# Second block of a two-block kernel: gate chain, output scaling and row product in another order on VectorE, w_hi one panel ahead at both norms, mean squares in two parts

## The chip, the cores and the metric

One core of a Trainium2 chip runs the whole kernel as one launch. The metric is the device time of an execution in microseconds (us); lower is better. The kernel before took 987.55 us, the median of three runs (987.34 to 988.13).

The engines are named as in the profile: PE is TensorE (matmuls), DVE is VectorE, ACT is ScalarE, POOL is GpSimd, SP issues most of the loads. Each works through its own queue of instructions in the order in which they were written, and waits on semaphores for the others.

## The reference, cut to what matters

The input is 256 tokens of 1024 features. A first block (modulated norm, gated spatial unit, state space scan, MLP) is followed by a second block. The change touches the end of the first block and the second one:

```
x = first_block(...)                     # ends with: rms_norm(x, final_norm_w)
xn = rms_norm_2(x, attn_norm_g)
proj = xn @ w_in                         # q, k, v of MoBA and GLA, gates; gate_lr is 16 wide
log_a = log_sigmoid(gate_lr @ w_gate_up + b_gate) / 16
og = gla_attention(gq, gk, gv, log_a)    # gated linear attention with decays exp(cumsum(log_a))
...                                      # MoBA attention, gating of og
x = x + concat([y_moba, y_gla]) @ w_out
hn = rms_norm_2(x, ffn_norm_g)
h = causal_dwconv(hn @ w_ffn_up, conv_w, conv_b)     # 3 taps, 5632 channels
x = x + (silu(h_gate) * h_val) @ w_ffn_down
return rms_norm_2(x, final_norm_g)
```

## The kernel before, in words

**Layout and weights.** Activations lie with features on the 128 partitions and the 256 tokens along the free axis. All large products are taken in three matmuls, since each operand is split into a high part in a reduced format and the rest: high x high, high x low, low x high (`panel`, L1443). The weights come as panels of 128 x 1024 numbers, four at a time in the slots of `raw`. For each panel SP loads `raw`, ACT converts it to `w_hi` (`split_hi`, L442), DVE subtracts to get `w_lo` (`split_lo`, L840), then PE takes it: 24 matmuls of 256 columns. `w_hi` of a slot may be written again once PE has finished the slot's former panel (semaphore `used`); `raw` once DVE has taken it (`taken`). A chunk is four panels, one output of 512 features for 256 tokens in half of `proj_ps`.

**Order.** It is written out by hand for each engine. Nothing is scheduled by a tool, so an instruction waits for all that stands ahead of it on its engine.

**The stage in2** (the second block's input projection; `i2` is its first chunk). So that PE need not wait for the norm, the first chunk is computed from unnormalised input (`pre2_hi`, `pre2_lo`) and scaled by the row of inverse root mean squares afterwards. The mean squares are matmuls with one column (`mean_square`, L1494, line of the matmul L1504); their inverse roots are put on a diagonal (`diag`, `broadcast`, L886) and spread over all partitions by one matmul with ones (`row_of`, L1509, matmul L1512); ACT copies the row to `rr_sb` (`row_scale`, L479). DVE and ACT then make the normalised input `act_hi`, `act_lo` in pairs of tiles (`norm_apply`, L894; `norm_hi`, L493), and in between each converts the next chunk's panels. There are two rows in this stage: row 2 is the second block's norm with the first block's final norm folded in, row 3 is the first block's final norm itself. Row 3 is used by `first_output` (L1221), which scales the residual `xres` in eight instructions, and is needed only when the second block's first residual is added, much later.

**The gate chain.** PE multiplies the 16 wide projection with `wgu` (L1761). DVE adds the bias and takes the absolute value (L1228, L1230), ACT takes exp(-|x|) (L724), DVE adds 1 (L1244), ACT takes the logarithm (L727) and exp of its negative (L729), DVE corrects rounding (`softplus_lost`, `softplus_add`, L919 to L923), forms log_sigmoid (L1250), divides by 16 (L1252) and takes a cumulative sum over the tokens (L1255, `glog`).

**The levels.** The decayed scores are computed in eight levels of block size 1 to 128. For level e DVE forms differences of `glog` in `gd` (`level_diff`, L1265), ACT takes exponentials (L719, L720), POOL multiplies queries and keys by them into `gx` (L424, L426), PE takes the level product (`level_mm`, L1788) and DVE picks the entries that belong to the level into `scores_t` (L1279). PE runs one level product behind each panel of the third and fourth chunk; product 0 uses `gqk` as it is, product 1 needs the first `gx`.

**The stage up** (`up`, eleven chunks) begins like in2: a first chunk from unnormalised input, mean squares, one row (row 4), the norm in pairs. Its first chunk is scaled into `up0` (L1392). Three convolution taps follow per chunk: the last one on ACT (`last_tap`, L566), the two earlier ones on DVE in two pairs of tiles (L1045), then a SiLU on ACT, the product on DVE (L1397) and the split into `glu_hi` and `glu_lo`. PE may write a half of `proj_ps` again once the taps of the chunk that lay there are done (`fc_done`).

## Time and profile before

| | |
|---|---|
| median of the runs | 987.55 us (987.34 to 988.13) |
| the profiled execution | 987.19 us |
| its span, first to last instruction | 985.5 us |
| busy, share of the span | PE 951.7 us (97%), DVE 696.0 (71%), ACT 528.2 (54%), POOL 149.8 (15%) |
| mean granted clock of PE | 0.983 of full speed |
| single operations, us | `w_lo` 1.2, next one 1.14 later; `w_hi` 1.05; table load on ACT 1.28; row copy on ACT 0.37; `diag` 0.42; `xres` scaling, 4 in a row, 1.65; memset of `scores_t` 1.34; memset of ones 0.48; scaling by 1/16 0.42; first `gd` 0.69 |
| a panel on PE at full clock | 24 matmuls, 0.12 us apart, some 2.9 us |

How to read it: the span is what the hardware profiler saw of one execution; about 1.7 us lie around it. In a timeline row the first number is the start in us from the span's start, the second the duration, xN says how many instructions a row merges, and the bracket at the end gives the engine's idle time before the row and whom it waited for. A duration of a matmul is longer than its distance to the next, since they are pipelined. The two passes of a matmul on full 32 bit numbers (mean squares, rows, level products) are counted one by one in the profile.

### The profile page before, as it was taken

Reading aid. Unit: us, or ns where it says so; the run is one execution under the profiler, and the core shown is the slowest. Engines: PE = TensorE matmul, PEld = TensorE weight load, DVE = VectorE, ACT = ScalarE, POOL = GpSimd, SP = SyncE. Lnnn points to the kernel's source line nnn. Section 1 sums busy time; section 2 is a strip of 40 time slices with the busy share of each in tenths; the row PEclk is TensorE's granted clock in tenths of the full one; section 3 lists DMA queues with packets and bytes.
Section 4 is the critical chain, followed back from the end, with each engine's and each line's share of the span. In section 5 each row is a group of like instructions: output and inputs, shape, how many; then the busy total and the mean of one; then the engine's idle time right before and its main releaser. Section 6 shows DMA issues by size and latency. Waiting matters only on the chain.

```text
span 985.5 us, 19172 instructions
## 1 busy us (share of the span) xinstructions
PE 951.7 (97%) x7452; PEld 902.4 (92%) x7452; DVE 696.0 (71%) x911; ACT 528.2 (54%) x715; POOL 149.8 (15%) x118
## 2 busy tenths in 40 slices
PE   8999999989999999999999999998998989999997
PEld 5799999979989899989999999987877989999996
DVE  5937877887899977566665454598765678877553
ACT  3466555555565664455555353564365666566442
POOL 0100000254786611000000020004300000000010
PEclk9999999999999999999999999998999999999999
DMA  9845445576676746535555646334323346556551
GB/s 347 340 154 167 152 171 175 170 253 195 223 244 219 235 165 194 190 129 183 179 170 179 206 149 209 116 127 136 121 86 107 108 142 195 182 187 183 193 200 43
DMA packets 54987, 175.53 MB, mean 178 GB/s; under 512 B 5440, under 2 KB 5840, under 8 KB 54928
## 3 DMA queue, kind: packets, MB, share of 16 engines
q1 hardware_dynamic: 53952, 172.39, 53.6%
q0 software_dynamic: 368, 1.31, 0.4%
q8 instruction: 42, 0.69, 0.3%
q10 hardware_dynamic: 608, 1.00, 0.3%
q14 instruction: 17, 0.14, 0.0%
HBM read 173.63 MB, written 1.05 MB: 177 GB/s over the span
## 4 chain that ended last, share of the span: by engine, by line
PE 66%; DVE 16%; ACT 8%; issue 5%; POOL 3%; DMA 2%; SPq 1%; ACTq 0%; DVEq 0%; POOLq 0%
PE proj_ps L1454 19%; PE proj_ps L1455 18%; PE proj_ps L1456 18%; DVE w_lo L842 4%; DVE conv_acc L1045 4%; ACT w_hi L446 3%; DVE mod_acc L854 3%; ACT conv_acc L566 1%; PE aux L1504 1%; PE proj_ps L1489 1%; ACT act_hi L497 1%; DMA mod_first<-in_panels 1%; PE proj_ps L1491 1%; PE proj_ps L1490 1%; DMA raw<-in_panels 1%
## 5 line engine op out<-in xcount | busy, mean ns | idle before, releaser
L842 DVE TENSOR_TENSOR w_lo<-raw,w_hi 128x1024 fp32r<-128x1024 f32 x276 | 352.5, 1288 | 192.1 <-ACT w_hi L446 191.7
L446 ACT CAST w_hi<-raw 128x1024 fp32r<-128x1024 f32 x276 | 286.3, 1046 | 248.4 <-PE proj_ps L1456 178.5
L1454 PE MATMUL proj_ps<-act_hi,w_hi 128*128 128x256 f32 x1280 | 368.9, 288 | 5.7 <-DVE w_lo L842 3.0
L1455 PE MATMUL proj_ps<-act_lo,w_hi 128*128 128x256 f32 x1280 | 365.0, 285 | 0.0
L1456 PE MATMUL proj_ps<-act_hi,w_lo 128*128 128x256 f32 x1280 | 364.8, 285 | 0.0
L1454 PEld LDWEIGHTS proj_ps<-act_hi,w_hi 128*128 128x128 f32 x1280 | 248.2, 194 | 12.1 <-issue 10.3
L1455 PEld LDWEIGHTS proj_ps<-act_lo,w_hi 128*128 128x128 f32 x1280 | 248.3, 194 | 0.7
L1456 PEld LDWEIGHTS proj_ps<-act_hi,w_lo 128*128 128x128 f32 x1280 | 248.1, 194 | 0.0
L410 POOL TENSOR_TENSOR tmp_b<-tmp_b 128x512 f32<-128x512 f32 x4 | 5.2, 1293 | 453.4 <-ACT tmp_b L469 453.4
L1454 PE MATMUL proj_ps<-ff_hi,w_hi 128*128 128x256 f32 x256 | 72.8, 284 | 0.0
L1455 PE MATMUL proj_ps<-ff_lo,w_hi 128*128 128x256 f32 x256 | 72.6, 284 | 0.0
L1456 PE MATMUL proj_ps<-ff_hi,w_lo 128*128 128x256 f32 x256 | 72.6, 284 | 0.0
L1454 PE MATMUL proj_ps<-glu_hi,w_hi 128*128 128x256 f32 x176 | 50.1, 284 | 0.0
L1456 PE MATMUL proj_ps<-glu_hi,w_lo 128*128 128x256 f32 x176 | 49.9, 284 | 0.0
L1455 PE MATMUL proj_ps<-glu_lo,w_hi 128*128 128x256 f32 x176 | 49.9, 283 | 0.0
L1455 PEld LDWEIGHTS proj_ps<-ff_lo,w_hi 128*128 128x128 f32 x256 | 49.2, 192 | 0.0
L1454 PEld LDWEIGHTS proj_ps<-ff_hi,w_hi 128*128 128x128 f32 x256 | 49.2, 192 | 0.0
L1456 PEld LDWEIGHTS proj_ps<-ff_hi,w_lo 128*128 128x128 f32 x256 | 49.2, 192 | 0.0
L854 DVE SCALAR_TENSOR_TENSOR mod_acc<-raw,silu_c,mod_acc 128x1024 f32<-128x1024 f32 x28 | 41.8, 1492 | 1.1 <-DMA raw<-in_panels 0.8
L1045 DVE SCALAR_TENSOR_TENSOR conv_acc<-proj_ps,cols,conv_acc 128x255 f32<-128x255 f32 (+2 forms) x96 | 38.8, 474 | 0.0
L1454 PE MATMUL proj_ps<-yb_hi,w_hi 128*128 128x256 f32 x128 | 36.7, 286 | 1.5 <-DVE w_lo L842 1.4
L1455 PE MATMUL proj_ps<-yb_lo,w_hi 128*128 128x256 f32 x128 | 36.3, 284 | 0.0
(334 smaller groups left out, 1661.7 us busy)
## 6 DMA issues: line engine op xcount, KB each, us to landing
raw<-in_panels SPq DMA_DIRECT2D x308, 512.0 KB, 3.7
mod_first<-in_panels SPq DMA_DIRECT2D x16, 512.0 KB, 10.7
xres<-in_x_t SPq DMA_DIRECT2D x2, 512.0 KB, 6.2
out_t<-tmp_a SPq DMA_DIRECT2D x4, 256.0 KB, 2.2
wst<-in_ws_t POOLq DMA_DIRECT2D x1, 512.0 KB, 3.8
bs_sb<-in_bs_rows POOLq DMA_DIRECT2D x1, 512.0 KB, 6.2
level_sb<-in_levels ACTq DMA_DIRECT2D x1, 512.0 KB, 4.2
cols<-in_cols SPq DMA_DIRECT2D x1, 267.0 KB, 2.9
```

The source lines that it names most:

```text
L446: nc.scalar.copy(w_hi[:, s, :], raw[:, s, :]).then_inc(hi_done, 1)
L497: nc.scalar.activation(act_hi[:, k], tmp_a[:, k], ACT.Identity, bias=shift(k)).then_inc(S["nrm_hi"], 1)
L566: ins = nc.scalar.activation(acc[:, c % 2, nt], tile_nt, ACT.Identity, bias=b(NT * c + nt), scale=w(NT * c + nt))
L842: tt(out=w_lo[:, s, :], in0=raw[:, s, :], in1=w_hi[:, s, :].bitcast(F32), op=ALU.subtract).then_inc(taken, 1)
L854: stt(out=mod_acc[:], in0=src, scalar=c_k, in1=mod_acc[:], op0=ALU.mult, op1=ALU.add).then_inc(done, 1)
L1045: ins = stt(out=out, in0=behind_nt, scalar=w(NT * c + nt, taps - 1 - back), in1=out, op0=ALU.mult, op1=ALU.add)
L1454: mm(dst, hi, xh, start=first and k == 0 and nt % 2 == 0, stop=False, skip_group_check=True)
L1455: mm(dst, hi, xl, start=False, stop=False, skip_group_check=True)
L1456: ins = mm(dst, lo, xh, start=False, stop=last and k == ks - 1, skip_group_check=True)
L1489: mm(dst, xh, wh, start=first and k == 0, stop=False)
L1490: mm(dst, xh, wl, start=False, stop=False)
L1491: ins = mm(dst, xl, wh, start=False, stop=last and k == 1)
```

## The change

On DVE: row 3's `diag` is made right behind row 2's release (before the norm); `first_output` moves from the gate chain into the second half of the level loop, two tiles behind each pick, and reads the row from `r1_sb`, to which ACT now copies it, and no longer from `aux`; the addition of 1 moves up to directly behind `gqk`; two `w_lo`, the memset of ones and `softplus_lost` stand before the wait for ACT's exponential; the third `w_lo` and the memset of `scores_t` come behind the first `gd`; the multiplication by 1/16 is gone and stands as scale of ACT's level exponentials. At both norms ACT converts the next chunk's panels one step earlier, the first ahead of the row copy. In up, also the first panel of the chunk after next is split by ACT and DVE before the taps. PE takes the panels of both first chunks in two halves; in in2 what stands between them is where it was, in up the mean squares 6 and 7 move half a panel behind the others, and the row half a panel later.

```diff
...
@@ -476,9 +477,9 @@
 
-            def row_scale(n):
+            def row_scale(n, dst):
                 act.wait_ge(S["rs_mm"], n)
-                nc.scalar.copy(rr_sb[:], aux[:, 3, 0:T]).then_inc(S["rr_ok"], 1)
+                nc.scalar.copy(dst, aux[:, 3, 0:T]).then_inc(S["rr_ok"], 1)
 
@@ -708,20 +709,22 @@
             root(3, stat[:, 3])
-            row_scale(2)
-            norm_hi(2, lambda k: zero8[:, k:k + 1], lambda k: split_hi(i2 + 1, k // 2) if k % 2 else None)
+            split_hi(i2 + 1, 0)
+            row_scale(2, rr_sb[:])
+            norm_hi(2, lambda k: zero8[:, k:k + 1], lambda k: split_hi(i2 + 1, (k + 1) // 2) if k in (1, 3, 5) else None)
 
             def level_exp(e):
 
                 m = (LEVELS + [P])[e]
                 view = gd[:, e % 2].rearrange("p (n m) -> p n m", m=2 * m)
                 act.wait_ge(S["lev_d"], e + 1)
-                nc.scalar.activation(view[:, :, m:2 * m], view[:, :, m:2 * m], ACT.Exp)
-                nc.scalar.activation(view[:, :, 0:m], view[:, :, 0:m], ACT.Exp, scale=-1.0).then_inc(S["lev_e"], 1)
+                nc.scalar.activation(view[:, :, m:2 * m], view[:, :, m:2 * m], ACT.Exp, scale=1.0 / 16)
+                nc.scalar.activation(view[:, :, 0:m], view[:, :, 0:m], ACT.Exp, scale=-1.0 / 16).then_inc(S["lev_e"], 1)
 
             split_hi(i2 + 2, 0)
             act.wait_ge(S["gx_abs"], 1)
             nc.scalar.activation(gt[:, 1], gt[:, 0], ACT.Exp, scale=-1.0).then_inc(S["gx_exp"], 1)
+            row_scale(3, r1_sb[:])
             split_hi(i2 + 2, 1)
@@ -798,8 +801,10 @@
             root(3)
-            row_scale(4)
-            norm_hi(3, lambda k: zero8[:, k:k + 1], lambda k: split_hi(up + 1, k // 2) if k % 2 else None)
+            split_hi(up + 1, 0)
+            row_scale(4, rr_sb[:])
+            norm_hi(3, lambda k: zero8[:, k:k + 1], lambda k: split_hi(up + 1, (k + 1) // 2) if k in (1, 3, 5) else None)
+            split_hi(up + 2, 0)
 
@@ -814,7 +819,8 @@
                 for s in range(SLOTS - 1):
-                    split_hi(up + c + 1, s)
+                    if (c, s) != (1, 0):
+                        split_hi(up + c + 1, s)
                     if s == 1:
@@ -1205,6 +1211,7 @@
             dve.wait_ge(S["rr_ok"], 1)
+            broadcast(3, stat[:, 2], wait=False)
 
@@ -1220,7 +1227,7 @@
                 for k in ks:
-                    last = stt(out=xres[:, k], in0=xres[:, k], scalar=col("final_norm_w", k), in1=rs_ps, op0=ALU.mult, op1=ALU.mult)
+                    last = stt(out=xres[:, k], in0=xres[:, k], scalar=col("final_norm_w", k), in1=r1_sb[:], op0=ALU.mult, op1=ALU.mult)
                 step(last)
@@ -1233,24 +1240,17 @@
             last.then_inc(evac_dve, 1)
-            split_lo(i2 + 1, 3)
-            dve.wait_ge(S["nrm_t"], 3 * KT)
-            broadcast(3, stat[:, 2], wait=False)
-            step(nc.vector.memset(scores_t[:], 0.0))
-            split_lo(i2 + 2, 0)
-            dve.wait_ge(S["rs_mm"], 3)
-            first_output(range(4))
             dve.wait_ge(S["gx_exp"], 1)
             ts(out=gt[:, 2], in0=gt[:, 1], scalar1=1.0, scalar2=None, op0=ALU.add).then_inc(S["gx_u"], 1)
+            split_lo(i2 + 1, 3)
+            split_lo(i2 + 2, 0)
+            dve.wait_ge(S["gx_u"], 1)
+            softplus_lost(gt[:, 1], gt[:, 2], gt[:, 0])
+            step(nc.vector.memset(gt[:, 1], 1.0))
             split_lo(i2 + 2, 1)
-            first_output(range(4, KT))
-            softplus_lost(gt[:, 1], gt[:, 2], gt[:, 0])
             dve.wait_ge(S["gx_inv"], 1)
             softplus_add(og2[:, 0:2], glog[:], gt[:, 0])
             step(stt(out=gt[:, 0], in0=og[:, 0:2], scalar=0.0, in1=glog[:], op0=ALU.min, op1=ALU.subtract))
-            split_lo(i2 + 2, 2)
-            step(ts(out=gt[:, 0], in0=gt[:, 0], scalar1=1.0 / 16, scalar2=None, op0=ALU.mult))
-            step(nc.vector.memset(gt[:, 1], 1.0))
             for t in range(2):
@@ -1283,7 +1283,10 @@
             level_diff(0)
+            split_lo(i2 + 2, 2)
+            step(nc.vector.memset(scores_t[:], 0.0))
             split_lo(i2 + 2, 3)
+            dve.wait_ge(S["rr_ok"], 2)
             for c in range(2):
@@ -1291,6 +1294,8 @@
                     level_pick(l)
+                    if c == 1:
+                        first_output((2 * s, 2 * s + 1))
 
@@ -1384,9 +1389,10 @@
             broadcast(4, stat[:, 1], wait=False)
-            dve.wait_ge(S["rr_ok"], 2)
+            dve.wait_ge(S["rr_ok"], 3)
             norm_apply(3, lambda k: col("ffn_g", k), lambda k: zero8[:, k:k + 1],
                        lambda k: split_lo(up + 1, k // 2) if k % 2 else None, rs=rr_sb[:])
+            split_lo(up + 2, 0)
             dve.wait_ge(used, (up + 1) * SLOTS)
...
@@ -1731,19 +1738,31 @@
 
-            def first_chunk(g, x_hi, x_lo, count, means, row):
+            def first_chunk(g, x_hi, x_lo, count, beside):
 
                 for s in range(SLOTS):
                     pe.wait_ge(S["pre_lo"], count + 2 * s + 2)
-                    panel(g, s, 0, x_hi, x_lo, 2 * s, s == 0, s == SLOTS - 1)
-                    if s == 0:
-                        means()
-                    if s == 1:
-                        row()
+                    for half in range(2):
+                        panel(g, s, 0, x_hi, x_lo, 2 * s, s == 0, s == SLOTS - 1, release=half, nts=(2 * half, 2 * half + 1))
+                        beside(s, half)
+
+            def beside_in2(s, half):
+                if (s, half) == (0, 1):
+                    mean_square(2, (6, 7), True)
+                if (s, half) == (1, 1):
+                    row_of(2)
+
+            def beside_up(s, half):
+                if (s, half) == (0, 1):
+                    mean_square(3, (0, 4, 5))
+                if (s, half) == (1, 0):
+                    mean_square(3, (6, 7))
+                if (s, half) == (2, 0):
+                    row_of(4)
 
             i2 = GROUP["in2"]
             pe.wait_ge(S["res_ok"], RES_FF2 + KT // 2)
-            first_chunk(i2, pre2_hi, pre2_lo, 0, lambda: mean_square(2, (6, 7), True), lambda: row_of(2))
+            first_chunk(i2, pre2_hi, pre2_lo, 0, beside_in2)
             pe.wait_ge(S["narrow_ok"], 2)
...
```

DVE in in2, from `gqk` on, before. `w_lo` is a panel's split, `gt`, `og` and `glog` are the gate chain, `gd` a level's differences:

```order
L1233 SCALAR_TENSOR_TENSOR gqk<-proj_ps,rr_sb 128x256 x3
L842 TENSOR_TENSOR w_lo<-raw,w_hi 128x1024 [waits hi_done]
L888 TENSOR_TENSOR diag<-square,stat 128x256 [waits nrm_t]
L1239 MEMSET scores_t 128x1536
L842 TENSOR_TENSOR w_lo<-raw,w_hi 128x1024 [waits hi_done,dve_step]
L1223 SCALAR_TENSOR_TENSOR xres<-xres,cols,aux 128x256 [waits rs_mm]
L1223 SCALAR_TENSOR_TENSOR xres<-xres,cols,aux 128x256 x3
L1244 TENSOR_SCALAR gt<-gt 128x512 [waits gx_exp,dve_step]
L842 TENSOR_TENSOR w_lo<-raw,w_hi 128x1024 [waits hi_done]
L1223 SCALAR_TENSOR_TENSOR xres<-xres,cols,aux 128x256 x4
L919 SCALAR_TENSOR_TENSOR gt<-gt 128x512 [waits dve_step]
L922 SCALAR_TENSOR_TENSOR gt<-gt,og_101 128x512 [waits gx_inv,dve_step]
```

The same place of the changed kernel, up to the first `gd`:

```order
L1240 SCALAR_TENSOR_TENSOR gqk<-proj_ps,rr_sb 128x256 x3
L1244 TENSOR_SCALAR gt<-gt 128x512 [waits gx_exp]
L848 TENSOR_TENSOR w_lo<-raw,w_hi 128x1024 [waits hi_done] x2
L925 SCALAR_TENSOR_TENSOR gt<-gt 128x512 [waits gx_u]
L1249 MEMSET gt 128x512 [waits dve_step]
L848 TENSOR_TENSOR w_lo<-raw,w_hi 128x1024 [waits hi_done,dve_step]
L928 SCALAR_TENSOR_TENSOR gt<-gt,og_101 128x512 [waits gx_inv]
L929 TENSOR_TENSOR glog<-glog,gt 128x512 [waits dve_step]
L1253 SCALAR_TENSOR_TENSOR gt<-og,glog 128x512 [waits dve_step]
L1255 SCALAR_TENSOR_TENSOR glog<-gt 128x256 [waits dve_step]
L1255 SCALAR_TENSOR_TENSOR glog<-gt 128x256
L1265 TENSOR_TENSOR gd<-glog 128x512 [waits dve_step]
```

Before, seven rows more (the rest of the chain with another `w_lo`, the scale and the memset of ones) stand between the last one shown and the first `gd`. Now `diag`, the memset of `scores_t`, both blocks of `xres` and one of the `w_lo` are gone from ahead of it, and `gt` (add 1) is first.

ACT at the same place, before. `gt`, `glog` and `og_101` are exp, logarithm and exp of the gate chain:

```order
L497 ACTIVATE act_hi<-tmp_a,zero_128 128x256 [waits nrm_t] x2
L446 CAST w_hi<-raw 128x1024 [waits used,landed_3]
L446 CAST w_hi<-raw 128x1024 [waits used,landed_0]
L724 ACT_TABLE_LOAD
L724 ACTIVATE gt<-gt 128x512 [waits gx_abs]
L446 CAST w_hi<-raw 128x1024 [waits used,landed_1]
L727 ACT_TABLE_LOAD
L727 ACTIVATE glog<-gt 128x512 [waits gx_u]
L729 ACT_TABLE_LOAD
L729 ACTIVATE og_101<-glog 128x512 [waits gx_ln]
```

And of the changed kernel, where `r_sb` is the new `r1_sb`:

```order
L498 ACTIVATE act_hi<-tmp_a,zero_129 128x256 [waits nrm_t] x2
L447 CAST w_hi<-raw 128x1024 [waits used,landed_0]
L726 ACT_TABLE_LOAD
L726 ACTIVATE gt<-gt 128x512 [waits gx_abs]
L482 COPY r_sb<-aux 128x256 [waits rs_mm]
L447 CAST w_hi<-raw 128x1024 [waits used,landed_1]
L730 ACT_TABLE_LOAD
L730 ACTIVATE glog<-gt 128x512 [waits gx_u]
L732 ACT_TABLE_LOAD
L732 ACTIVATE og_101<-glog 128x512 [waits gx_ln]
```

The copy of row 3 is new between the first exponential and the `w_hi` ahead of the logarithm; one `w_hi` fewer stands between the norm's `act_hi` and the first exponential.

DVE in up, from the norm's last pair to the first chunk's taps, before. `up_116` is `up0`:

```order
L898 SCALAR_TENSOR_TENSOR tmp_a<-xres,cols,rr_sb 128x256 x2
L903 SCALAR_TENSOR_TENSOR act_lo<-tmp_a,zero_128,act_hi 128x256 [waits nrm_t,nrm_hi] x2
L842 TENSOR_TENSOR w_lo<-raw,w_hi 128x1024 [waits hi_done]
L1392 TENSOR_TENSOR up_116<-proj_ps,rr_sb 128x256 [waits used]
L1392 TENSOR_TENSOR up_116<-proj_ps,rr_sb 128x256 x3
L1045 SCALAR_TENSOR_TENSOR fconv_acc<-up_116,cols,fconv_acc 128x255 [waits ftap_act,evac_dve]
L1045 SCALAR_TENSOR_TENSOR fconv_acc<-up_116,cols,fconv_acc 128x255 [waits ftap_act]
L1045 SCALAR_TENSOR_TENSOR fconv_acc<-up_116,cols,fconv_acc 128x254 [waits ftap_dve] x2
L842 TENSOR_TENSOR w_lo<-raw,w_hi 128x1024 [waits hi_done]
L1045 SCALAR_TENSOR_TENSOR fconv_acc<-up_116,cols,fconv_acc 128x255 [waits evac_act] x2
L1045 SCALAR_TENSOR_TENSOR fconv_acc<-up_116,cols,fconv_acc 128x254 [waits ftap_dve] x2
```

And of the changed kernel:

```order
L904 SCALAR_TENSOR_TENSOR tmp_a<-xres,cols,rr_sb 128x256 x2
L909 SCALAR_TENSOR_TENSOR act_lo<-tmp_a,zero_129,act_hi 128x256 [waits nrm_t,nrm_hi] x2
L848 TENSOR_TENSOR w_lo<-raw,w_hi 128x1024 [waits hi_done] x2
L1398 TENSOR_TENSOR up_117<-proj_ps,rr_sb 128x256 [waits used]
L1398 TENSOR_TENSOR up_117<-proj_ps,rr_sb 128x256 x3
L1051 SCALAR_TENSOR_TENSOR fconv_acc<-up_117,cols,fconv_acc 128x255 [waits ftap_act,evac_dve]
L1051 SCALAR_TENSOR_TENSOR fconv_acc<-up_117,cols,fconv_acc 128x255 [waits ftap_act]
L1051 SCALAR_TENSOR_TENSOR fconv_acc<-up_117,cols,fconv_acc 128x254 [waits ftap_dve] x2
L1051 SCALAR_TENSOR_TENSOR fconv_acc<-up_117,cols,fconv_acc 128x255 [waits evac_act] x2
L1051 SCALAR_TENSOR_TENSOR fconv_acc<-up_117,cols,fconv_acc 128x254 [waits ftap_dve] x2
L848 TENSOR_TENSOR w_lo<-raw,w_hi 128x1024 [waits hi_done]
```

A second `w_lo` stands ahead of `up0`, and none is left between the two pairs of taps; the `w_lo` behind both pairs is that of the chunk's second panel, as before.

## Rows read from the trace of the kernel before

**Rows 1.** The page, busy time (share of the span) and instructions
```profile
PE 951.7 (97%) x7452; PEld 902.4 (92%) x7452; DVE 696.0 (71%) x911; ACT 528.2 (54%) x715; POOL 149.8 (15%) x118
```

**Rows 2.** Waits of PE: who waited for whom, us in total, times, longest
```profile
PE aux L1788 <- POOL gx L426: 4.4, 1, 4.4
PE proj_ps L1454 <- DVE w_lo L842: 4.3, 3, 2.5
...
PE aux L1512 <- DVE diag L888: 1.7, 1, 1.7
```

**Rows 3.** Stretches: span, PE, PEld, DVE, ACT, POOL busy, granted clock, DMA, GB/s
```profile
620.00:669.00 49.00, 44.10 (x365) 42.35 (x364) 40.04 (x71) 29.34 (x45) 1.03 (x2) 1.00 0.38 119
...
669.00:675.80 6.80, 5.63 (x33) 5.41 (x34) 6.80 (x9) 2.42 (x5) 5.12 (x5) 0.50 0.55 163
...
781.70:785.20 3.50, 3.50 (x17) 3.37 (x17) 1.03 (x3) 0.00 (x0) 0.00 (x0) 0.51 0.79 261
...
805.80:809.00 3.20, 3.19 (x15) 3.20 (x16) 3.20 (x7) 2.41 (x3) 0.00 (x0) 0.50 0.51 164
```

**Rows 4.** Timeline of PE in in2: the row, then level products 1 to 3
```profile
652.29 0.70 PE L1512 MATMUL aux<-diag,ones 128*128 128x256 f32 x2 [1.68 <-DVE diag L888]
...
670.17 2.08 PE L1788 MATMUL aux<-gx 64*128 64x128 f32 x16 [4.39 <-POOL gx L426]
...
676.86 1.16 PE L1788 MATMUL aux<-gx 64*128 64x128 f32 x16
...
681.02 1.16 PE L1788 MATMUL aux<-gx 64*128 64x128 f32 x16
```

**Rows 5.** Timeline of DVE in in2, gate chain and levels
```profile
649.36 1.41 DVE L1233 SCALAR_TENSOR_TENSOR gqk<-proj_ps,rr_sb 128x256 f32<-128x256 f32 x4
...
656.70 0.43 DVE L1244 TENSOR_SCALAR gt<-gt 128x512 f32<-128x512 f32 x1
...
660.59 0.69 DVE L922 SCALAR_TENSOR_TENSOR gt<-gt,og 128x512 f32<-128x512 f32 x1
...
662.77 1.23 DVE L842 TENSOR_TENSOR w_lo<-raw,w_hi 128x1024 fp32r<-128x1024 f32 x1
...
665.03 1.27 DVE L1255 TENSOR_TENSOR_SCAN glog<-gt 128x256 f32<-128x256 f32 x2
666.33 0.69 DVE L1265 TENSOR_TENSOR gd<-glog 128x512 f32<-128x512 f32 x1
...
668.08 1.33 DVE L1265 TENSOR_TENSOR gd<-glog 128x512 f32<-128x512 f32 x1
...
690.58 1.22 DVE L842 TENSOR_TENSOR w_lo<-raw,w_hi 128x1024 fp32r<-128x1024 f32 x1 [1.06 <-ACT w_hi L446]
```

**Rows 6.** Timeline of ACT and POOL in in2: logarithm, first gx's second product
```profile
657.16 0.63 ACT L727 ACTIVATE glog<-gt 128x512 f32<-128x512 f32 x1 [4.12 <-DVE gt L1244]
...
668.83 1.28 POOL L426 TENSOR_TENSOR gx<-gqk,gd 128x256 f32<-128x256 f32 x1
```

**Rows 7.** Chain that ended last: start, us, what (mean squares of in2)
```profile
630.05 1.68 PE aux L1504 x16
```

**Rows 8.** Timeline of PE in up: mean squares, the third chunk's first panel
```profile
778.11 2.29 PE L1504 MATMUL aux<-avg_d,tmp_b 128*128 128x1 f32 x20
...
805.80 0.55 PE L1454 MATMUL proj_ps<-act_hi,w_hi 128*128 128x256 f32 x1 [2.54 <-DVE w_lo L842]
```

**Rows 9.** Timeline of DVE in up: norm's first split, taps, splits
```profile
788.19 1.23 DVE L842 TENSOR_TENSOR w_lo<-raw,w_hi 128x1024 fp32r<-128x1024 f32 x1 [0.45 <-ACT w_hi L446]
...
802.58 1.67 DVE L1045 SCALAR_TENSOR_TENSOR fconv_acc<-up,cols,fconv_acc 128x255 f32<-128x255 f32 x4 [1.23 <-ACT fconv_acc L566]
...
807.15 1.21 DVE L842 TENSOR_TENSOR w_lo<-raw,w_hi 128x1024 fp32r<-128x1024 f32 x1
...
816.26 1.65 DVE L1045 SCALAR_TENSOR_TENSOR fconv_acc<-proj_ps,cols,fconv_acc 128x255 f32<-128x255 f32 x4
```

More of the change, by code:

```diff
@@ L181, in two_blocks @@
         rr_sb = at("rr_sb", 152, [T])
+        r1_sb = at("r1_sb", 153, [T])
         pre2_hi = at("pre2_hi", 136, [KT, T], F32R)
@@ L1417, in _ @@
                         glu_low(c - 1)
-                    split_lo(up + c + 1, s)
+                    if (c, s) != (1, 0):
+                        split_lo(up + c + 1, s)
             for g in range(1, 3):
```

2 lines of the change are left out of this document (1 added, 1 removed).

## The prediction, written before the changed kernel was run

> **What bounds the kernel now.** I read the shares of busy time first, then PE's own waits, then the granted clock by stretches, then PE's timeline around each wait and the engine that it waits for. PE is busy for 97% of the span [rows 1], so only three things can give time back: its waits, stretches at the lower of its two clock levels, and work removed from it. Nothing is removed here. Three entries of its list of waits lie where the change works [rows 2]: one matmul that spreads a row waits 1.7 us for `diag`, one level product waits 4.4 us for `gx`, and of the three waits for `w_lo` the longest, 2.5 us, is in the second block's up projection. The clock adds to them [rows 3]: it is 1.00 between 620 and 669 us, 0.50 from 669 to 675.8, right behind the 4.4 us wait, and again about 0.5 in 781.7 to 785.2 and 805.8 to 809.0. That is 1.2 GHz instead of 2.4. Before the second of these spells PE worked 2.29 us on twenty passes of one column (the mean squares), before the third it waited 2.54 us [rows 8].
>
> **Part 1: the row and the gate chain (in2).** The wait for the row goes. Its `diag` was made behind a `w_lo` late in the stage; now it stands right behind the first row's release, before the norm's products. It costs VectorE some 0.4 us there, which is covered, since the step behind waits for the product with `wgu` on PE (0.3 us of the norm's own idle time also goes). Gain 1.68 us [rows 4].
>
> The wait for `gx` is a question of when VectorE's first `gd` (level 0) is made. It starts at 666.33, and PE starts again at 670.17, 3.84 us later, through exponentials on ACT and two products on POOL [rows 4, 5]. The steps before it, moved one by one [rows 5] (durations of single operations are in the table of the profile):
> - `gqk` starts at 649.36 and stays there. `gt<-gt` (L1244) started at 656.70, behind two `w_lo`, `diag`, the memset of `scores_t` and four `xres`; now it is next after `gqk`, at about 650.8.
> - ACT's logarithm started at 657.16, 0.46 us after L1244 [rows 6]. It can't move by the same 5.9 us: ACT now has the copy of the row to `r1_sb` ahead of it, which waits for PE's row at about 650.5 + 0.6, then a `w_hi` (1.0) and a table load (1.28). I get 653.8, 3.35 us earlier. The exponential behind it then ends near 656.4.
> - `gt<-gt,og` (L922) started at 660.59, 0.85 us after that exponential had ended, since `softplus_lost` came late; now that one runs beforehand, and L922 starts at 656.45, 4.15 us earlier.
> - From there to the scan, the stretch from 662.77 to 665.03 (a `w_lo`, the scaling by 1/16, the memset of ones: 2.26 us) leaves the path. The scale is free in ACT's exponential, and the memset now fills the wait for ACT. Scan and `gd` follow: 666.33 - 4.15 - 2.26 = 659.9.
>
> So `gx` is there at 659.9 + 3.84 = 663.8. PE, without its two waits, wants it at 670.17 - 4.39 - 1.68 = 664.1. The wait is gone, with 0.3 us to spare. What is late next is level 1: its `gd` stands behind two `w_lo`, the memset of `scores_t` and one `gd`, so it starts at about 659.9 + 0.7 + 1.14 + 1.36 + 1.14 = 664.3 and is with PE at 668.1; PE wants it 4.16 us after the first (the distance 676.86 to 681.02 [rows 4]), at 668.3. Equal within my error. With the wait goes the spell at 0.50: from 670.17 to 676.86 PE needed 6.69 us for what takes it 4.16 later, 2.53 us more [rows 4]. The sum of part 1: 1.68 + 4.39 + 2.53 = 8.6 us. Bounds: if `gx` or level 1 comes 1 us late and half such a spell follows, 6.2; if the start of the stage also gains its 0.3, 8.9. I take 8.5, near the rows' own sum, since both needed times come out just ahead.
>
> The four pairs of `first_output` now stand in the second half of the level loop. A pair costs 0.8 us (the block of four took 1.65), and the hole in front of each `w_lo` there is 1.06 us, VectorE waiting for ACT, which waits for PE [rows 5]. Covered. Without that cover it would be 4 x 0.8 us on VectorE, but level products there are made a whole panel ahead of use, so PE would still not see it.
>
> On the products of POOL there is something to weigh. VectorE's second `gd` took 1.33 us and POOL's product beside it 1.28 us, while the first `gd` took 0.69 [rows 5, 6]. The Trainium skill, "SBUF — State Buffer", section on who interferes with whom, says that a VectorE operation with two SBUF inputs and a GpSimd operation that reads SBUF exclude each other for a whole instruction. By that rule the first products would now meet a `w_lo` and then a memset, which reads nothing, instead of a `w_lo` and a `gd`; the first `gx` would come some 0.5 us sooner, and `first_output`, whose row now comes from SBUF and no longer from PSUM, could hold POOL up later. By the rows the sum stays as it is: the first is time to spare already, the second falls in slack.
>
> **Part 2: the second norm (up).** Means: twenty passes in a block become twelve and eight with half a panel between. The block of sixteen in in2 took 1.68 us [rows 7], and the clock stayed at 1.00 behind it [rows 3], so I expect no spell at 781.7. It cost PE about 1.6 us (3.5 us at 0.51 [rows 3], less the half that was done anyway). The row is issued half a panel later but at full clock, so ACT's copy and the norm start at the same time.
>
> VectorE's rounds in the norm each wait 0.45 us for `w_hi` [rows 9]; one panel ahead, the four waits go: 1.8 us. One more `w_lo` (1.14) now stands ahead of `up0`, so the taps start 0.66 us sooner than 802.58. PE's short wait for the norm's last `w_lo` (0.4 us) shrinks and that of 2.54 at 805.80 goes [rows 8]. But the next panel's `w_lo` is not moved past the taps: it ended at 807.15 + 1.21 = 808.36 [rows 9] and will end at 808.36 - 0.66 - 1.14 - 0.18 = 806.4. PE, which now starts the chunk near 801.1, is at that panel at 804.1 and waits 2.3 us. Before, it came there at 810.2, slowed by the third spell. Up to here 3.8 us are gained. Then the third chunk waits for the second chunk's taps. They ended at 816.26 + 1.65 = 817.9 [rows 9], a full 1 us before PE needed them at 818.9; all of ACT and VectorE behind that `w_lo` moves up by 2.0, to 815.9, and PE would be there at 815.1. So 3.0 us remain if the clock holds through the new wait; with a spell behind it (as behind the old one of 2.54) PE is there at 816.5 and 2.4 remain. I take 2.7. Bounds: 1.5 (the means' spell stays and delays the row and with it the norm by 1.2) and 3.8. From there VectorE does a chunk in 10.7 us against PE's 11.6, so nothing more is lost.
>
> **Sum.** 8.5 + 2.7 = 11.2 us. The profiled execution took 985.5 us of span and 1.7 around it, 987.2, 0.36 under the median of the runs shown, 987.55. I forecast 976.0 for an execution like the profiled one and 976.3 for the median.
>
> **Rivals.**
> - The stall comes back at level 0 or 1. For it: my two margins are 0.3 and 0.2 us, and POOL's products varied between 0.7 and 1.6 us. Against: POOL meets less VectorE work there than before. One wait of 1 us and a spell of up to 2.5: 976.3 + 3 = 979.3.
> - Part 2 pays little, since VectorE's chain sets the end there and not the wait that was removed: the spell at the means stays, the norm starts 1.2 us later. 1.2 to 1.5 us remain: 977.7. For it: twelve and eight passes with 1.4 us between are still close together.
> - Nothing goes wrong at the taps, because ACT and VectorE run further ahead than I think: PE takes up all it lost in part 2, near 5 us: 974.
> - Clock spells fall elsewhere. There is a fourth one in the stages between, behind another block of one-column products. The Trainium skill, "TensorE: Matmul & The Clock Gate", Part 1, says that the chip's look at PE's activity is free-running and doesn't start with the kernel, so such spells may move from run to run. What one costs is in the rows, 1.5 to 2.5 us: up to 978.5. The runs shown lie within 0.8 us of one another, so this is not large.
> - The other side, slower: the clock. If the new pattern, level products of half width and shorter waits between panels, held PE at 1.2 GHz through in2's third and fourth chunk, 192 matmuls at up to twice their 0.12 us, up to 23 us would come on top: 999. It decides from about 13 us of extra on, some 110 matmuls at the low clock. For it: a spell of 6.8 us followed one wait [rows 3]. Against: the same alternation of panels and level products ran at full clock from 676 us on, and there are now fewer waits in front.
>
> **How the numbers follow.** My forecast (974.8 to 978) 0.65; stall back 0.13; little in part 2 0.09; more at the taps 0.05; spells elsewhere 0.05; slower 0.03. The rival cases up to 980 lie inside the range 974.4 to 980.2, which leaves out the slow case, part of the case at 974, and combinations of two rivals, some 0.15. A difference of under 0.2% (2 us) is one that a measurement of this kernel can't tell from none; a gain under 2 us would need several rivals at once, 0.03. Faster 0.94, same 0.03, slower 0.03.
>
> **What would show it.** In the changed profile: the row behind in2's second panel has no wait; the first level product from `gx` follows its panel with at most 0.3 us idle, the clock stays 1.00 through that stretch, and the distance from it to the next is 4.2 us; no spell follows the mean squares of up; the 2.5 us wait of the chunk's first panel is gone and one of about 2.3 us stands at its second, with perhaps a spell behind it; the third chunk waits up to 0.9 us for the taps. It would be wrong if the first `gd` started less than 5 us sooner against the stage's start, if a wait of 1 us or more stood at the level products, or if PE's second panel of that chunk did not wait.

## The result, and the profile of the changed kernel

The changed kernel took 980.39 us, the median of four runs (979.28 to 981.61), against 987.53 (987.34 to 988.13) for the kernel before on the same chip: a ratio of 0.9927, 95% interval 0.991 to 0.9944, that is 7.1 us faster (5.5 to 8.9). A second comparison, in e5, gave 0.9928 (0.9902 to 0.9953). The forecast was 976.3 us; the median lies 0.2 us above the upper end of the range (980.2). The profiled execution took 979.56 us, with a span of 977.8.

I cut both traces at the same instructions of PE; the stretches are differences of the starts in its timeline. "Products 1 and 2" are the first two level products that use `gx`; the "first score product" is the first matmul of `k_sb` with `q_sb`; the "late mean squares" are the first of the last stage (957.05 us before; some expectations below call them the last mean squares but one).

| stretch | before | after | gained |
|---|---|---|---|
| start to in2's first panel | 627.01 | 626.12 | 0.89 |
| A: to product 1 | 43.16 | 36.75 | 6.41 |
| B: to product 2 | 6.69 | 4.16 | 2.53 |
| C: to the first score product | 40.05 | 44.11 | -4.06 |
| D: to up's first panel | 58.32 | 59.09 | -0.77 |
| E: to the late mean squares | 181.82 | 179.19 | 2.63 |
| F: to the end | 28.45 | 28.38 | 0.07 |

A and B are the gate chain's, 8.94 us. C is the surprise. PE's waits first, who waited for whom (us in total, times, longest), from the changed kernel:

```profile
PE proj_ps L1461 <- DVE w_lo L848: 3.4, 2, 2.0
PE aux L1828 <- DVE scores_t L1279: 2.4, 1, 2.4
```

The waits for `gx` (4.4) and `diag` (1.7) of [rows 2] have gone. The second line above is new. In PE's timeline, the row of in2, products 1 and 2, the turn product (the matmuls that rotate q, the rope) and the second panel of up's third chunk:

```profile
649.56 0.60 PE L1519 MATMUL aux<-diag,ones 128*128 128x256 f32 x2
...
662.87 0.38 PE L1807 MATMUL aux<-gx 64*128 64x128 f32 x2
...
667.03 1.16 PE L1807 MATMUL aux<-gx 64*128 64x128 f32 x16
...
694.93 2.61 PE L1828 MATMUL aux<-q_sb,square 128*128 128x256 f32 x7 [2.35 <-DVE scores_t L1279]
...
800.98 0.35 PE L1461 MATMUL proj_ps<-act_hi,w_hi 128*128 128x256 f32 x1 [2.03 <-DVE w_lo L848]
```

The first three have no bracket: no wait, where [rows 4] had 1.68 at the row and 4.39 at product 1. The turn product waits for the last pick into `scores_t`. DVE's timeline shows why that is late:

```profile
658.92 0.69 DVE L1265 TENSOR_TENSOR gd<-glog 128x512 f32<-128x512 f32 x1
...
683.17 0.86 DVE L1230 SCALAR_TENSOR_TENSOR xres<-xres,cols,r_sb 128x256 f32<-128x256 f32 x2
...
687.32 2.99 DVE L1230 SCALAR_TENSOR_TENSOR xres<-xres,cols,r_sb 128x256 f32<-128x256 f32 x2
690.34 3.30 DVE L848 TENSOR_TENSOR w_lo<-raw,w_hi 128x1024 fp32r<-128x1024 f32 x1
693.56 1.31 DVE L1279 COPY_PREDICATED scores_t<-level_sb,aux 128x512 f32<-128x512 uint32 x2
```

A pair of `first_output` (L1230) takes 0.86 us, the third takes 2.99. A `w_lo` takes 1.2 [rows 5], this one 3.30. POOL at that time:

```profile
687.39 2.63 POOL L433 TENSOR_TENSOR rope_c<-q_sb,rope_sb 128x1024 f32<-128x1024 f32 x1
689.99 2.57 POOL L433 TENSOR_TENSOR rope_c<-k_sb,rope_sb 128x1024 f32<-128x1024 f32 x1
```

The pair's second instruction ends at 690.31, 0.3 us after POOL's product of q (690.02), and the `w_lo` at 693.64, 1.1 us after its product of k (692.56): about what each needs by itself, once POOL is out of the way. The clock by stretches (span, PE, PEld, DVE, ACT, POOL busy, granted clock, DMA, GB/s) adds the rest:

```profile
640.00:694.90 54.90, 52.58 (x466) 48.58 (x464) 52.27 (x72) 32.05 (x46) 18.90 (x18) 1.00 0.44 142
694.90:698.50 3.60, 3.57 (x10) 2.93 (x11) 3.06 (x5) 0.00 (x0) 0.00 (x0) 0.61 0.49 158
770.20:786.00 15.80, 15.80 (x134) 15.74 (x133) 11.86 (x22) 11.10 (x21) 1.35 (x2) 1.00 0.39 116
801.00:806.00 5.00, 5.00 (x29) 5.00 (x30) 3.29 (x4) 4.83 (x9) 0.00 (x0) 0.66 0.66 199
```

At full clock from 640 us until the new wait, partly at 1.2 GHz behind it, full through up's means and norm, partly low again behind the wait of 2.03. So C lost 2.35 us of waiting and 1.7 of clock.

### The profile page after: what moved, and what is told of

Its sections match the earlier page's. It is cut to its first block, busy times and chain, and to the rows that moved or that the text cites. A ratio compares the mean times of both kernels' runs of the same rounds, so it can differ in the third digit from the quotient of the medians.

```text
span 977.8 us, 19174 instructions
## 1 busy us (share of the span) xinstructions
PE 947.6 (97%) x7452; PEld 898.8 (92%) x7452; DVE 696.1 (71%) x910; ACT 528.5 (54%) x716; POOL 149.6 (15%) x118
## 4 chain that ended last, share of the span: by engine, by line
PE 72%; DVE 13%; ACT 5%; issue 4%; POOL 3%; DMA 1%; SPq 1%; POOLq 0%; DVEq 0%; ACTq 0%
PE proj_ps L1461 20%; PE proj_ps L1462 20%; PE proj_ps L1463 20%; DVE conv_acc L1051 4%; DVE w_lo L848 3%; ACT w_hi L447 2%; DVE mod_acc L860 1%; ACT conv_acc L567 1%; PE aux L1511 1%; PE aux L1524 1%; DMA mod_first<-in_panels 1%; POOL a_upto_lo L374 1%; PE proj_ps L1496 1%; POOL a_upto_hi L372 1%; PE aux L1807 1%
## 5 line engine op out<-in xcount | busy, mean ns | idle before, releaser
L1461 PEld LDWEIGHTS proj_ps<-act_hi,w_hi 128*128 128x128 f32 x1280 | 246.6, 193 | 10.8 <-issue 8.9
```

The source lines that it names most:

```text
L1461: mm(dst, hi, xh, start=first and k == 0 and nt % 2 == 0, stop=False, skip_group_check=True)
```

## The experiments

Two theories on C. Collision: POOL's long products and DVE instructions with two inputs in SBUF exclude each other. Load: DVE simply has too much to do there. On up: are the spells (stretches in which PE is granted 1.2 instead of 2.4 GHz) bound to the block of twenty passes, or do they come and go? Ratios are to the kernel before, with 95% intervals; C, D and E are the stretches of the table above. In these comparisons the runs of the kernel before ranged from 982.2 to 989.3 us, so medians that differ by less than 2 us are not told apart, and the stretches decide.

| | ratio (interval) | C | D | E |
|---|---|---|---|---|
| e1 pairs behind the ropes | 0.9891 (0.9873 to 0.9909) | 40.05 | 60.74 | 178.62 |
| e2 row from PSUM | 0.9908 (0.9886 to 0.9929) | 40.05 | 57.58 | 178.60 |
| e3 part 1 alone | 0.9953 (0.9934 to 0.9971) | 44.13 | 59.08 | 179.62 |
| e4 part 2 alone | 0.9988 (0.9973 to 1.0002) | 40.04 | 58.30 | 178.64 |
| e5 changed kernel again | 0.9928 (0.9902 to 0.9953) | 44.16 | 61.02 | 179.19 |
| e6 POOL's rope products later | 0.9928 (0.9906 to 0.995) | 41.59 | 60.82 | 179.18 |
| e7 panels ahead in up | 0.9874 (0.9853 to 0.9895) | 40.05 | 59.09 | 176.88 |
| e8 means in one block | 0.9941 (0.9923 to 0.9959) | 44.12 | 59.09 | 179.21 |
| e9 row half a panel earlier | 0.9865 (0.9843 to 0.9888) | 40.05 | 58.32 | 177.17 |
| e10 all together | 0.9866 (0.9842 to 0.989) | 40.05 | 59.10 | 175.44 |
| e11 scale by 1/16 back | 0.9954 (0.9936 to 0.9973) | 44.18 | 60.89 | 179.19 |
| e12 before again | one run, 986.61 us | 40.05 | 58.31 | 181.73 |

### C: e1, e2, e6

e1 takes the two last pairs out of the loop:

```diff
-                    if c == 1:
+                    if c == 1 and s < 2:
                         first_output((2 * s, 2 * s + 1))
...
             rope(0, q_sb)
+            first_output((4, 5))
             split_lo(i2 + 5, 1)
             rope(1, k_sb)
             split_lo(i2 + 5, 2)
+            first_output((6, 7))
```

> The changed kernel with one move: the third and fourth pair of first_output leave the level loop; the third stands behind the first rope, the fourth behind the last w_lo but one of that stage. Collision theory: in the changed kernel the third pair (687.32, 2.99 us for two instructions that take 0.88 elsewhere) ran beside POOL's rope product of q (687.39 to 690.02), and because the pair used the gap between POOL's two rope products, the next w_lo (3.30 instead of 1.2) had to wait for POOL's product of k as well. With the pair gone from there the w_lo takes the gap, the last pick starts some 2.4 us sooner, PE's wait of 2.35 us at the turn product goes, and so does the low clock behind it (about 1.6 us): 980.4 - 4.0 = 976.4 us. Rival, a loaded VectorE (any work in these panels makes the last pick late): the move relieves it as well, same time, so this run does not separate the two. Rival, the time is lost again behind (the score products wait, or a clock spell comes elsewhere): 978.5 to 980.

Measured: C is 40.05 again, to the hundredth what it is in the kernel before; 4.06 us are back and no wait stands at the turn product. D was long in this execution (60.74, a spell at 718 to 724), so the trace's total gained less than C; the ratio gives 10.8 us under the kernel before. e2 tells the theories apart:

```diff
+                    if c == 1 and s == 2:
+                        for k in (4, 5):
+                            last = stt(out=xres[:, k], in0=xres[:, k], scalar=col("final_norm_w", k), in1=aux[:, 0, 0:T],
+                                       op0=ALU.mult, op1=ALU.mult)
```

The edit also makes PE's next level product wait for the pair. What stands in that bank is not the row, so the scaling of these two tiles is left out as such; the amount of work is the same.

> The changed kernel, with the third pair of first_output where it is, but its row operand read from a bank of PSUM in place of r1_sb. It takes other numbers as the row for two tiles (that scaling is left out as such), and PE's ninth level product waits for the pair. Collision theory, in its narrow form (only an instruction with two SBUF inputs is held up by POOL): the pair takes about 0.9 us although POOL's rope product of q runs beside it, the w_lo behind it is the next to take the gap between POOL's two products and ends near 691.2, the last pick is in time, PE's wait at the turn product is under 0.3 us: 976.4. Wide form (any VectorE instruction that reads SBUF is held up): pair near 3 us, wait of 2.3 us, 980.4. Loaded VectorE: the same amount of work stands at the same place, so 980.4 and a wait of about 2.3 us, with no single instruction stretched by more than before.

DVE, then POOL, in e2:

```profile
688.50 0.88 DVE L1299 SCALAR_TENSOR_TENSOR xres<-xres,cols,aux 128x256 f32<-128x256 f32 x2
690.34 1.71 DVE L848 TENSOR_TENSOR w_lo<-raw,w_hi 128x1024 fp32r<-128x1024 f32 x1 [0.96 <-ACT w_hi L447]
...
693.23 1.74 DVE L1230 SCALAR_TENSOR_TENSOR xres<-xres,cols,r_sb 128x256 f32<-128x256 f32 x2
```

```profile
688.59 2.38 POOL L433 TENSOR_TENSOR rope_c<-q_sb,rope_sb 128x1024 f32<-128x1024 f32 x1
690.92 3.37 POOL L433 TENSOR_TENSOR rope_c<-k_sb,rope_sb 128x1024 f32<-128x1024 f32 x1
```

With one of the two tensors in PSUM the pair takes 0.88 us while POOL's product runs, and that product takes 2.38, as in the kernel before. The `w_lo`, with both in SBUF, is held for 0.5 us until the product of q ends (690.97), and then POOL's product of k is the one that is held: 3.37 instead of 2.38. The fourth pair, still from SBUF, is held until that one ends (694.29). Same work on DVE, no wait on PE, C 40.05: the load theory is out. So is the wide form of the collision. e6 leaves DVE alone and moves POOL:

```diff
+            pool.wait_ge(S["lev_ok"], 8)
             for w, x in enumerate((q_sb, k_sb)):
```

> The changed kernel, with POOL's two rope products held back until the pick of level product 7 is done (one wait more on POOL, nothing moved on VectorE). Collision theory: the third pair of first_output takes 0.88 instead of 2.99 us and the w_lo behind it 1.2 instead of 3.30; the fourth pair or the w_lo behind it meets POOL instead and is stretched, where PE does not wait for it. From level product 2 to the first score product 40.05 us as before and not 44.1: 4.0 us under the changed kernel, 976.4 if that is 980.4. Loaded VectorE: VectorE's work is the same, so the wait stays and the stretch stays at 44.1.

DVE, and PE's product for k, in e6:

```profile
692.49 2.96 DVE L1231 SCALAR_TENSOR_TENSOR xres<-xres,cols,r_sb 128x256 f32<-128x256 f32 x2
695.49 3.31 DVE L849 TENSOR_TENSOR w_lo<-raw,w_hi 128x1024 fp32r<-128x1024 f32 x1
```

```profile
699.46 0.48 PE L1829 MATMUL aux<-k_sb,square 128*128 128x256 f32 x1 [1.25 <-DVE scores_t L1274]
```

The stretching follows POOL's products to the fourth pair and the next `w_lo`, with the same sizes (2.96 and 3.31). The collision theory holds, but I was wrong that PE would not see it there: the copy behind that `w_lo` came late by 1.25 us, and C is 41.59, not 40.05. The ratio doesn't show the 2.5 us that C gained: it is 0.9928, that of the changed kernel in e5, where 4.0 us had been expected. For e6 the stretches alone speak.

### The parts alone, and the margins: e3, e4, e5, e11

e3 takes in2 from the changed kernel and up from the one before; e4 the other way round, from these same lines (e3 against the changed kernel):

```diff
-            split_hi(up + 1, 0)
             row_scale(4, rr_sb[:])
-            norm_hi(3, lambda k: zero8[:, k:k + 1], lambda k: split_hi(up + 1, (k + 1) // 2) if k in (1, 3, 5) else None)
-            split_hi(up + 2, 0)
+            norm_hi(3, lambda k: zero8[:, k:k + 1], lambda k: split_hi(up + 1, k // 2) if k % 2 else None)
...
-            split_lo(up + 2, 0)
...
                 if (s, half) == (0, 1):
-                    mean_square(3, (0, 4, 5))
-                if (s, half) == (1, 0):
-                    mean_square(3, (6, 7))
-                if (s, half) == (2, 0):
+                    mean_square(3, (0, 4, 5, 6, 7))
+                if (s, half) == (1, 1):
                     row_of(4)
```

> Part 1 alone: everything of in2 as in the changed kernel, everything of up as before. From the traces: 8.9 us gained at the level products, 4.0 lost at the turn product and behind it, 0.8 more up to the stage up: 987.5 - 4.1 = 983.4 us. If the prediction's 8.5 us had held: 979.0. If part 2's gain depends on part 1 (both use the same slack), more than 983.4 is not expected but the sum of the two single gains differs from 7.1 by over 1 us.

> Part 2 alone: in2 as before, up as in the changed kernel (means in two parts, w_hi and w_lo ahead at the norm). From the traces 2.6 us are gained between the first chunk of up and 830 us, where 2.7 had been forecast: 984.9. Rival, little in part 2 (the spell after the means stays, or another comes): 986.2. No wait of 2.5 us at the third chunk's first panel, one of about 2.0 at its second.

e3 gained 4.6 us by its ratio (2.9 to 6.5); 8.94 less 4.06 is 4.88. e4 gained 1.2 (-0.2 to 2.7), where the traces had promised 2.6: that is the case of the rival, little in part 2. Its waits were as expected, none of 2.5 us at the third chunk's first panel and 2.04 at its second. Together 5.8, and both parts 7.1 (5.5 to 8.9): they add up within the error. D is 59.08 in e3, as in the changed kernel's first profile, but no edit's (e5, below). And e3's trace of up, where all code is that of the kernel before, holds something that I had not expected. Its clock around the block of twenty passes and behind its wait of 2.52 us, and the same stretch of e12:

```profile
774.00:780.00 6.00, 6.00 (x53) 5.95 (x52) 4.00 (x7) 3.29 (x7) 0.00 (x0) 1.00 0.34 111
800.20:812.00 11.80, 11.75 (x96) 11.57 (x96) 10.08 (x18) 7.74 (x11) 0.00 (x0) 1.00 0.52 181
```

```profile
779.90:784.00 4.10, 4.10 (x25) 4.10 (x25) 2.38 (x5) 0.78 (x2) 0.00 (x0) 0.64 0.57 161
```

In e3 neither spell of [rows 3] is there, and E is 179.62 instead of 181.82. Against that, E with part 2 is 178.6 in e1, e2 and e4, at a clock of 1.00 from 786 to 945 us in all three and in e3: without clock spells the second part is worth 1.0 us.

> The kernel before once more, for one look at its clock. If the low clock behind the twenty passes of one column and behind the wait of 2.54 us in up belonged to the program, both are there again, and the distance from the first panel of up to the last mean squares but one is 181.8 us. If they come and go from execution to execution, as e3 suggests (same code in up, none of the two, 179.6), it lies somewhere between 179.6 and 181.8.

The kernel before once more has the spell behind the means (0.64) and E 181.73. In both of its profiles the spells are there, in e3 none.

> The changed kernel itself once more, beside the three others of this set on one chip. By the first comparison 0.9927 of the kernel before. By the traces of e3 and e4 (8.94 us gained up to level product 2, 4.06 lost at the turn product, 1.0 gained in up where no clock spell falls): 5.9 us, a ratio of 0.994. In the trace: the wait of 2.3 us at the turn product again, since it hangs on the order and not on chance; the clock spells behind one-column products at other places or absent.

e5 has C 44.16 again, and D 61.02 where the first profile of the same kernel had 59.09. The clock of the same stretch of time, first profile, then e5:

```profile
721.40:726.30 4.90, 4.28 (x19) 2.95 (x18) 4.21 (x8) 4.86 (x13) 0.00 (x0) 1.00 0.25 81
```

```profile
721.40:726.30 4.90, 4.84 (x17) 3.92 (x18) 4.22 (x9) 4.84 (x12) 0.00 (x0) 0.65 0.19 52
```

So one program has a spell in one execution and not in the next. D has two places for one: behind the sixteen one-column passes on `og` (718.93 in the changed kernel's first profile) and behind the wait of 1.74 us for `mix_lo` (736.10 there). The granted clock of the ten us at each sorts all fourteen profiles: D is 57.6 with no spell (e2), 58.3 with the first alone (before, e4, e9, e12), 59.1 with the second alone (the changed kernel's first profile, e3, e7, e8, e10), 60.7 to 61.0 with both (e1, e5, e6, e11). e11 puts 0.42 us back on the gate chain (and takes the scale of 1/16 out of ACT's exponentials):

```diff
+            step(ts(out=gt[:, 0], in0=gt[:, 0], scalar1=1.0 / 16, scalar2=None, op0=ALU.mult))
```

> The changed kernel with the multiplication by 1/16 back on VectorE ahead of the scan (0.42 us more on the gate chain). In the changed kernel POOL ends the first gx 0.59 us before PE starts its product (662.28 against 662.87), the second 0.13 us before (666.90 against 667.03). If the chain's terms add up as the prediction has them: first product without a wait, a wait of about 0.3 us at the second, and with it at most 0.5 us of the median; no spell, since the wait is short. If instead there is hidden slack behind (VectorE's memset or ACT set the second gx), no wait at all: equal to the changed kernel.

```profile
669.07 0.38 PE L1808 MATMUL aux<-gx 64*128 64x128 f32 x2 [0.33 <-POOL gx L427]
```

No wait at product 1, 0.33 us at product 2, B 4.56 instead of 4.16: the chain's terms add up as the prediction has them, and 0.13 us of margin was all there was. The median was missed: the ratio is 0.0027 above that of the changed kernel, some 2.6 us, where 0.5 at most was expected and the trace shows 0.4 in B. Its profiled execution has both spells in D (60.89). The intervals overlap (0.9936 to 0.9953); whether more than chance is in it stays open.

### up: e8, e9, e7, e10

e8 has all twenty passes in one block again:

```diff
-                    mean_square(3, (0, 4, 5))
-                if (s, half) == (1, 0):
-                    mean_square(3, (6, 7))
+                    mean_square(3, (0, 4, 5, 6, 7))
```

> The changed kernel, with all twenty passes of one column of up in one block again, as before. As the prediction has it, the spell of 3.5 us at the low clock follows such a block, and not the block of twelve: 1.6 us slower than the changed kernel, row and norm 1.2 us later. Rival, from the trace of e3, where the same block of twenty passes had no spell behind it: the spells come and go from execution to execution whatever stands there, the profile shows one or none, and the median moves by 0.2 to 0.8 us.

No spell followed the block, and E is 179.21 against 179.19: the rival was right. Of four profiles with a block of twenty (before, e12, e3, e8), two had the spell; of ten with twelve and eight, none. That the split helps is possible, but not shown. e9 puts the row where it was, on top of e1:

```diff
-                if (s, half) == (2, 0):
+                if (s, half) == (1, 1):
                     row_of(4)
```

> e1 (pairs behind the ropes) with the row of up put back behind the second panel of the first chunk, where it stood in the kernel before; the change has it half a panel later. Counted from the first panel of up, VectorE's norm starts at +9.02 us in e3 (up as before, no clock spell), at +10.55 in the kernel before (spell behind the means) and at +10.46 wherever the row is half a panel later (e4, e7). Theory: without a spell, the later row gives back 1.44 of the 1.8 us that the four w_hi waits had cost, and this is why part 2 was worth 1.0 us and not 2.7. So the norm starts at +9.0, the wait of 2.03 us at the second panel falls to about 0.6, the distance from the first panel to the last mean squares but one from 178.6 to 177.2: 1.4 us under e1. Rival: diag is late for the earlier place, PE waits for it there: nothing gained.

The norm's first instruction on DVE in the changed kernel (up begins at 770.23), in e9 (765.48), and e9's wait at the second panel:

```profile
780.69 0.48 DVE L904 SCALAR_TENSOR_TENSOR tmp_a<-xres,cols,rr_sb 128x256 f32<-128x256 f32 x1 [2.83 <-ACT rr_sb L482]
```

```profile
774.50 0.48 DVE L904 SCALAR_TENSOR_TENSOR tmp_a<-xres,cols,rr_sb 128x256 f32<-128x256 f32 x1 [1.39 <-ACT rr_sb L482]
```

```profile
794.78 0.36 PE L1463 MATMUL proj_ps<-act_hi,w_hi 128*128 128x256 f32 x1 [0.58 <-DVE w_lo L848]
```

It starts at +10.46 in the one and at +9.02 in the other, the wait of 2.03 is 0.58, E is 177.17 where 177.2 was expected. The later row did cost 1.44 us. e7 (on e1) splits the third chunk's panels before what they don't depend on:

```diff
             split_hi(up + 2, 0)
+            split_hi(up + 2, 1)
...
                 glu_high(c - 1)
+                if c == 1:
+                    split_hi(up + 2, SLOTS - 1)
...
+            split_lo(up + 2, 1)
             dve.wait_ge(evac_dve, 6)
```

> e1 (pairs behind the ropes) and, in up, all four panels of the chunk after next ahead of what they do not depend on: w_hi and w_lo of its second panel before the taps (VectorE idles 1.23 us there), of its third before the SiLU, w_hi of its fourth before the next chunk's last tap. The wait of 2.03 us at the second panel goes, and VectorE's taps of the second chunk end 1.7 us earlier (ACT's last tap no longer waits in front of that w_lo); the third chunk then waits about 1.0 us for them instead of 0.67. Sum: 1.8 us under e1. Rival, VectorE's own chain sets the end of the third chunk whatever the order of the panels: the wait only moves to that chunk, under 0.5 us gained. Without clock spells the distance from the first panel of up to the last mean squares but one was 178.6 us in e1, it should be 176.8.

E 176.88 (176.8 expected), no wait at the second panel, 1.19 us at the next chunk for its taps. e10 adds e9's edit and this on ACT, with `glu_low(0)` behind the fourth panel's `split_lo` on DVE:

```diff
-                glu_high(c - 1)
                 if c == 1:
                     split_hi(up + 2, SLOTS - 1)
+                glu_high(c - 1)
```

> e7 with two edits more: the row half a panel earlier as in e9, and w_hi and w_lo of the second chunk's fourth panel ahead of glu_hi and glu_lo of the first (VectorE idled 0.69 and 0.26 us there in e7, the third chunk waited 1.19 for the taps). All waits of PE in up's first three chunks go: from the first panel of up to the last mean squares but one 176.88 - 1.19 = 175.7 us; 1.2 us under e7, a ratio of 0.986. Rival, glu_lo late or the taps' other inputs set the time: 176.3 or more.

PE has no wait left in up before 830 us and E is 175.44 (175.7 expected). The ratio, 0.9866, is that of e9 and 0.0008 under e7: the last 1.7 us of E don't show in the medians. e9 and e10 beat both kernels: 13 us under the kernel before, 6 under the changed one.

## Why the prediction was wrong

- **The row and the gate chain: right.** The row has no wait. The first `gd` starts 32.80 us behind in2's first panel instead of 39.32, 6.5 us sooner (6.4 forecast). Product 1 had 0.59 us to spare (POOL ended its `gx` at 662.28, PE took it at 662.87; 0.3 forecast, and POOL's second product took 0.86 us instead of the 1.28 of [rows 6]), product 2 0.13 us (0.2 forecast). No spell. A and B gave 8.94 us, where the sum was 8.6 and 8.5 was taken.
- **"Covered", of the four pairs of first_output: this step failed.** The prediction put 0.8 us a pair into a hole of 1.06 and said that even without cover "PE would still not see it". For three pairs the price holds: seven of the eight instructions took under 0.5 us. The eighth, the second of the third pair, took 2.6. That pair ran into POOL's rope products, took 2.99 us in all, let POOL's second product go ahead of the next `w_lo`, and so made the last pick late by more than the panel of slack: 2.35 us of waiting and 1.7 of clock, 4.06 in all. e1 and e2 each take it away whole. I had looked at the level loop in its steady part and not at what POOL does at its end, although the trace before had the collision in small (DVE, then POOL):

```profile
698.90 1.78 DVE L842 TENSOR_TENSOR w_lo<-raw,w_hi 128x1024 fp32r<-128x1024 f32 x1 [1.64 <-ACT w_hi L446]
```

```profile
697.23 2.38 POOL L432 TENSOR_TENSOR rope_c<-q_sb,rope_sb 128x1024 f32<-128x1024 f32 x1
699.56 3.37 POOL L432 TENSOR_TENSOR rope_c<-k_sb,rope_sb 128x1024 f32<-128x1024 f32 x1
```

- The `w_lo` took 0.6 us more than the others and waited for the gap between POOL's products; POOL's second took 1.0 more than its first. The prediction did weigh the rule on this (the Trainium skill, "SBUF — State Buffer", section on who interferes with whom) and even named `first_output`, but with POOL as the one held up, and closed with "falls in slack". By that rule the third pair and the `w_lo` are each held until an instruction of POOL has ended, and the trace agrees: each took 2.1 us longer beside a product of 2.6 and ended 0.3 and 1.1 us after it. The same section of the Trainium skill says that a VectorE operation with at most one SBUF input doesn't meet GpSimd (outside its two port modes); e2 agrees, with 0.88 us.
- **Part 2: the sum right, its terms not.** E gave 2.63 us, 2.7 forecast. But 1.6 us of PE's time was booked on the means' spell, and with it the unchanged start of the norm, and the block of twenty passes ran without one in e3 and e8. "ACT's copy and the norm start at the same time" was true only beside an execution with the spell (+10.55); without it the norm started at +9.02, and the row half a panel later cost 1.44 us of the 1.8 that the `w_hi` waits gave. Between executions without spells the part is worth 1.0 us, and 1.2 (-0.2 to 2.7) by e4's ratio. The new wait at the second panel came as forecast (2.03 for 2.3); the third chunk's wait, up to 0.9 forecast, was 0.67 in e1, e2 and e4, and none in the changed kernel's profile, behind a spell.
- **The rivals.** No stall at levels 0 and 1, and no slow clock through the chunks. "Part 2 pays little" is what the experiments show, though not by a spell that stays. "Spells elsewhere" happened beside the rest: D was 0.77 us longer, and ranged over 57.6 to 61.0 in the fourteen profiles, 59.1 and 61.0 for the changed kernel alone. In D the changed kernel's first profile lost the one spell of the kernel before and had the other, dearer one. No case had a new wait on DVE by way of POOL, and the range ended 0.2 us too low. None of the signs of being wrong that the prediction names appeared: they watch the first `gd`, the level products and up, and the loss fell behind the levels. The case of the stall is also mis-added (a wait of 1 us and a spell of up to 2.5 make 3.5, not 3), though 979.8 would still lie in the range.
- **The sum.** 8.94 - 4.06 - 0.77 + 2.63 + 0.07 = 6.8 us in the traces behind in2's first panel, where 11.2 was forecast; the medians give 7.1. With the failed step undone (e1) the ratio of 0.9891 makes 976.8 of the 987.53 us. That this meets the forecast of 976.3 is partly luck, since part 2 had been put 1.7 us too high.

## What to carry to other kernels

Before work with two SBUF operands is moved on VectorE, lay GpSimd's timeline beside the new place, over its whole length: here an instruction of under 0.5 us was held by a GpSimd product of 2.6, and the gap that it took afterwards was one that the next critical instruction didn't get. Moving the pair away, or reading one operand from PSUM, gave all of it back. And a term that rests on a spell at the low clock is not the edit's until a second execution shows the spell too: price each step of such a chain against an execution without one.

## What the runs showed of the hardware

- VectorE instructions with two inputs in SBUF and GpSimd's products exclude each other for whole instructions, in both directions. Held on VectorE: a pair of 0.88 us took 2.99, a subtraction of 1.2 us took 3.30. Held on GpSimd: a product of 2.38 us took 3.37. An instruction that already waited took the gap between two of GpSimd's (the second of the pair in the changed kernel, the `w_lo` in e2 and in the kernel before).
- Spells at 1.2 GHz in one and the same program: the changed kernel had one at 721.4 to 726.3 us in e5 and none there in its first profile. Behind the wait of 2.35 us at the turn product one followed in all five profiles that have the wait (C 44.11 to 44.18); behind the 2.52 us of e3 in up and the 1.25 us of e6, none. Behind the wait of 1.74 us in D one followed in nine of fourteen profiles, behind the sixteen one-column passes there in eight. What decides between them stays open. The Trainium skill, "TensorE: Matmul & The Clock Gate", Part 1, has the chip's look at PE as free-running; the difference between e5 and the first profile agrees with that. That a part of it hangs on the program is not shown: the kernel before had the same spells in both of its profiles, but two are few.
